# VectorE makes the low weight halves at both ends of a layer, GpSimd scales every second mixer tile, and each product sum takes its high weights first

## What is computed

```python
for l in range(2):
    proj = rmsnorm(x, norm1_g[l]) @ w_in[l]                 # 1024 -> q, k, v, hyena inputs, gates
    a_out = neighbourhood_attention(q, k, v, na_rpb[l])     # 8 heads of 64, with softmax
    u = short_conv(hy_in, ...)                              # width 3, per channel
    b_out = hyena_mixer(u, h_fwd, h_bwd, hy_bias[l])        # long convolutions by spectra
    merged = g0 * (a_out @ w_up_na[l]) + g1 * (b_out @ w_up_hy[l])
    x = x + merged @ w_out[l]
    h = rmsnorm(x, norm2_g[l])
    q = h @ peer_wq[l]; s = q . subkeys                     # scores, top 16 of 128, twice, top 16 of all
    a = gelu(h @ peer_u[l].T)                               # all 16384 experts are computed here
    x = x + (routing weights * a) @ peer_v[l]
```

## Time and profile before

| | us |
|---|---|
| median of 3 runs | 1931.53 |
| lowest and highest | 1929.2 and 1931.96 |
| profiled execution, its own time | 1929.89 |
| its span, first to last instruction | 1927.8 |
| PE busy | 1873.0 (97%) |
| ACT busy | 1355.3 (70%) |
| DVE busy | 1218.7 (63%) |
| POOL busy | 1035.3 (54%) |

### The profile page before, as it was taken

How to read it: one execution, slowest core, us unless ns; L and a number is a source line. 1 busy time by engine, 2 the same in 40 slices (tenths; PEclk the granted TensorE clock), 3 DMA queues, 4 the chain that set the end, 5 groups by cost and what they waited for, 6 DMA issues and landing times.

```text
span 1927.8 us, 42946 instructions
## 1 busy us (share of the span) xinstructions
PE 1873.0 (97%) x14238; PEld 1353.3 (70%) x14238; DVE 1218.7 (63%) x2530; ACT 1355.3 (70%) x1929; POOL 1035.3 (54%) x664
## 2 busy tenths in 40 slices
PE   7989999999999999999989899999999989999999
PEld 5777898899998344444457778988999974444444
DVE  5897569777775344444458974796777744444444
ACT  8787988887777455555588879888877765555554
POOL 4655868876667322222256558687776672222221
PEclk8999999999999999999999999999999999999999
DMA  8544656655555566666565446556555555656654
GB/s 265 164 143 142 214 168 201 202 188 173 174 174 167 173 205 203 200 206 200 192 213 167 143 135 227 173 197 201 192 171 167 173 175 175 206 201 202 206 198 140
DMA packets 100324, 357.38 MB, mean 185 GB/s; under 512 B 11744, under 2 KB 13730, under 8 KB 99492
## 3 DMA queue, kind: packets, MB, share of 16 engines
q1 hardware_dynamic: 99828, 354.36, 55.9%
q10 hardware_dynamic: 432, 2.18, 0.3%
HBM read 355.45 MB, written 1.05 MB: 185 GB/s over the span
## 4 chain that ended last, share of the span: by engine, by line
PE 87%; DVE 6%; ACT 5%; issue 2%; DMA 0%; SPq 0%; POOL 0%; DVEq 0%; ACTq 0%; POOLq 0%
PE bank L1992 35%; PE bank L1536 14%; PE bank L1538 14%; PE bank L1540 14%; PE bank L1931 3%; ACT w_hi L504 2%; ACT ring L510 2%; PE bank L1860 1%; DVE arena L1150 1%; DVE arena L1167 1%; PE bank L1911 1%; PE bank L1865 1%; DVE arena L1146 1%; DVE arena L1148 1%; PE bank L1699 0%
## 5 line engine op out<-in xcount | busy, mean ns | idle before, releaser
L462 POOL TENSOR_TENSOR w_lo<-ring,w_hi 128x1024 f16<-128x1024 f32 x404 | 863.9, 2140 | 396.5 <-ACT ring L510 395.9
L504 ACT ACTIVATE w_hi<-ring 128x1024 f16<-128x1024 f32 x654 | 685.0, 1047 | 38.2 <-PE bank L1540 25.2
L1536 PE MATMUL bank<-act_parts,w_hi 128*128 128x256 f16 x2560 | 698.0, 273 | 0.5 <-DVE act_parts L1268 0.5
L1540 PE MATMUL bank<-act_parts,w_lo 128*128 128x256 f16 x2560 | 697.8, 273 | 0.0
L1538 PE MATMUL bank<-act_parts,w_hi 128*128 128x256 f16 x2560 | 697.7, 273 | 0.0
L897 DVE SCALAR_TENSOR_TENSOR w_lo<-ring,w_hi 128x1024 f16<-128x1024 f32 x250 | 306.3, 1225 | 351.7 <-ACT w_hi L504 351.7
L476 POOL TENSOR_TENSOR e_lo<-arena,e_hi 128x256 f16<-128x256 f16 x256 | 171.2, 670 | 480.9 <-ACT e_hi L813 480.9
L510 ACT ACTIVATE ring<-ring 128x1024 f32<-128x1024 f32 x404 | 424.2, 1050 | 0.0
L1992 PE MATMUL bank<-w_hi,e_hi 128*128 128x512 f16 x1024 | 390.3, 381 | 11.3 <-issue 11.3
L1992 PE MATMUL bank<-w_lo,e_hi 128*128 128x512 f16 x1024 | 390.2, 381 | 0.0
L1992 PE MATMUL bank<-w_hi,e_lo 128*128 128x512 f16 x1024 | 389.9, 381 | 0.0
(11 more groups left out here) (258 smaller groups left out, 1862.1 us busy)
## 6 DMA issues: line engine op xcount, KB each, us to landing
ring<-stream SPq DMA_DIRECT2D x654, 512.0 KB, 3.3
arena<-rpb_in SPq DMA_DIRECT2D x8, 512.0 KB, 6.2
arena<-subkeys ACTq DMA_DIRECT2D x2, 1024.0 KB, 5.6
ring<-stream SPq DMA_DIRECT2D x4, 256.0 KB, 4.8
xT<-x_in SPq DMA_DIRECT2D x4, 256.0 KB, 5.2
arena<-w_in SPq DMA_DIRECT2D x2, 512.0 KB
arena<-decay_in SPq DMA_DIRECT2D x2, 512.0 KB
arena<-dft_in SPq DMA_DIRECT2D x2, 512.0 KB, 4.3
```

The lines of the kernel that those rows point to most:

```text
L462: pool.tensor_tensor(w_lo[:, slot, :], ring[:, slot, :], w_hi[:, slot, :], ALU.subtract).then_inc(lo_ready.sem, 1)
L504: nc.scalar.activation(w_hi[:, slot, :], ring[:, slot, :], ACT.Copy, scale=TABLE_SCALE).then_inc(hi_ready.sem, 1)
L1536: T.matmul(out_, weights(w_hi, tile, j), hi[:, k, :], start=start, stop=False, skip_group_check=True)
L1540: return T.matmul(out_, weights(w_lo, tile, j), hi[:, k, :], start=False, stop=stop, skip_group_check=True)
```

## The change

Three things are changed.

1. **DVE makes the low halves at both ends of a layer.** Tiles 2 to 5 of each layer, and tiles 200 to 203, move from POOL to DVE's one-instruction form, and ACT no longer scales them. DVE's `low_part` for tiles 2 and 3 stands in layer 0 behind the second and fourth `add_squares`, in layer 1 behind the second and fourth `raw_low_pair`; for tiles 4 and 5 behind the sum of squares, ahead of `inverse_rms`. For tiles 200 to 203 it stands among the last three `store_late`. DVE's wait for the low half of tile 203 is gone. POOL begins with tile 6 and ends with tile 199.
2. **POOL scales the odd tiles from 7 to 71 itself.** There it waits for `hi_ready`, scales the tile in place with a `tensor_scalar`, waits for itself, and subtracts. ACT scales 33 tiles fewer in each layer this way. The even tiles from 6 to 70, and all of 72 to 199, stay as they were. That makes 404 scalings on ACT before, 322 after, and 66 new ones on POOL.
3. **`contract` takes high weights first.** It waits for the high half, issues the 16 matmuls with `w_hi` (both activation halves, block by block), then waits for the low half and issues the eight with `w_lo`. The number of matmuls is the same. At tile 4 the mean of squares is behind the wait for the high half, and no longer behind that for the low half.

`lo_ready` is split in `low_by_vector` and `low_by_pool`, each counted in its own order; PE and SP wait for the one of the tile's maker. Loops are cut where the maker changes.

```diff
+VECTOR_HEAD = 6
+def made_by_vector(tile):
+    return tile < VECTOR_HEAD or tile >= T_VT
+def scaled_by_pool(tile):
+    return VECTOR_HEAD <= tile < T_U and tile % 2 == 1
...
+        def low_wait(eng, l, i, tile):
+            made = low_by_vector if made_by_vector(tile) else low_by_pool
+            eng.wait_ge(made.sem, made.at(l, i * RING + lows_by_engine(tile)))
...
-            def scaled_low(l, i, tile):
+            def pool_low(l, i, tile):
                 slot = tile % RING
-                pool.wait_ge(ring_scaled.sem, ring_scaled.at(l, i * RING + (tile + 1 - HEAD)))
+                if scaled_by_pool(tile):
+                    pool.wait_ge(hi_ready.sem, hi_ready.at(l, tile + 1))
+                    scaled[0] += 1
+                    pool.tensor_scalar(ring[:, slot, :], ring[:, slot, :], TABLE_SCALE, None, ALU.mult
+                                       ).then_inc(pool_scaled, 1)
+                    pool.wait_ge(pool_scaled, scaled[0])
+                else:
+                    pool.wait_ge(ring_scaled.sem, ring_scaled.at(l, i * RING + scaled_by_scalar(tile)))
                 pool.tensor_tensor(w_lo[:, slot, :], ring[:, slot, :], w_hi[:, slot, :], ALU.subtract
-                                   ).then_inc(lo_ready.sem, 1)
+                                   ).then_inc(low_by_pool.sem, 1)
             def pool_layer(l):
-                pool.wait_ge(lo_ready.sem, lo_ready.at(l, HEAD))
-                for tile in range(HEAD, RING):
-                    scaled_low(l, 0, tile)
-                with pool.Fori(1, POOL_TILES // RING) as i:
+                for tile in range(VECTOR_HEAD, T_U):
+                    pool_low(l, 0, tile)
+                with pool.Fori(0, NK // RING) as i:
                     for s in range(RING):
-                        scaled_low(l, i, s)
+                        pool_low(l, i, T_U + s)
...
             def scale_tile(tile):
+                if not made_by_vector(tile) and not scaled_by_pool(tile):
...
                         raw_low_pair(b)
                         if not l:
                             head_low(b % 2, b // 2)
+                        elif b % 2:
+                            low_part(l, 0, HEAD + b // 2)
                 for b in range(KT // 2):
                     add_squares(b, pair_sum, bank[6 + b % 2][:, :])
+                    if not l and b % 2:
+                        low_part(l, 0, HEAD + b // 2)
...
+                for tile in range(RING, VECTOR_HEAD):
+                    low_part(l, 0, tile)
                 inverse_rms(1)
...
                 burst(TGROUPS // RING - 1, False)
+                low_part(l, 0, T_VT)
                 store_late(0, LATE - 3)
-                dve.wait_ge(lo_ready.sem, lo_ready.at(l, POOL_TILES))
+                low_part(l, 0, T_VT + 1)
                 for n in range(LATE - EDGE, LATE):
                     store_late(0, n, last_fresh)
+                    low_part(l, 0, T_VT + RING + n - LATE)
...
                 def contract(out_, i, tile, wait=None, parts=(act_hi, act_lo)):
-                    parts_ready(i, tile)
+                    hi, lo = parts
+                    high_ready(i, tile)
                     for k in range(KT):
                         if wait is not None:
                             wait(k)
-                        ins = product(out_, tile, k, k, k == 0, k == KT - 1, parts)
+                        for moving in (hi, lo):
+                            T.matmul(out_, weights(w_hi, tile, k), moving[:, k, :], start=(k == 0 and moving is hi),
+                                     stop=False, skip_group_check=True)
+                    parts_ready(i, tile)
+                    for k in range(KT):
+                        ins = T.matmul(out_, weights(w_lo, tile, k), hi[:, k, :], start=False, stop=(k == KT - 1),
+                                       skip_group_check=True)
                     return ins
```

More of the change, by code:

```diff
@@ L89, with lows_by_engine, scaled_by_scalar @@
 PI_BELOW = 3.1415925
+def made_by_vector(tile):
+    return tile < VECTOR_HEAD or tile >= T_VT
+def scaled_by_pool(tile):
+    return VECTOR_HEAD <= tile < T_U and tile % 2 == 1
+def lows_by_engine(tile):
+    return sum(made_by_vector(t) == made_by_vector(tile) for t in range(tile + 1))
+def scaled_by_scalar(tile):
+    return sum(not made_by_vector(t) and not scaled_by_pool(t) for t in range(tile + 1))
 class Signal:
@@ L272, in encoder_kernel @@
         hi_ready = sig("hi_ready", TILES)
-        ring_scaled = sig("ring_scaled", POOL_TILES - HEAD)
-        lo_ready = sig("lo_ready", TILES)
+        ring_scaled = sig("ring_scaled", scaled_by_scalar(TILES - 1))
+        low_by_vector = sig("low_by_vector", lows_by_engine(TILES - 1))
+        low_by_pool = sig("low_by_pool", lows_by_engine(T_VT - 1))
+        pool_scaled = sem("pool_scaled")
         tile_done = sig("tile_done", TILES)
@@ L365, in load, with refill @@
                              ).then_inc(ring_full[slot].sem, 16)
-            def refill(turn, slot):
-                sp.wait_ge(lo_ready.sem, turn * RING + (slot + 1 - RING))
-                load(turn * RING + slot, slot)
+            def refill(l, i, group, slot):
+                tile = (group - 1) * RING + slot
+                if group:
+                    low_wait(sp, l, i, tile)
+                else:
+                    low_wait(sp, l - 1, i, TILES + tile)
+                load(i * RING + (l * TILES + group * RING + slot), slot)
             def layer_loads(l):
@@ L410, in layer_loads @@
                     for slot in (2 * (r % 2), 2 * (r % 2) + 1):
-                        refill(l * GROUPS + 3 + r // 2, slot)
+                        refill(l, 0, 3 + r // 2, slot)
                         if slot % 2 == 0:
                             offsets(r)
-                with sp.Fori(l * GROUPS + 5, (l + 1) * GROUPS) as turn:
+                with sp.Fori(0, T_VT // RING + 1 - 5) as i:
                     for slot in range(RING):
-                        refill(turn, slot)
+                        refill(l, i, 5, slot)
+                with sp.Fori(0, GROUPS - 1 - T_VT // RING) as i:
+                    for slot in range(RING):
+                        refill(l, i, T_VT // RING + 1, slot)
             def load_x(b):
@@ L509, in scale_tile @@
                 slot = tile % RING
-                nc.scalar.activation(ring[:, slot, :], ring[:, slot, :], ACT.Copy, scale=TABLE_SCALE
-                                     ).then_inc(ring_scaled.sem, 1)
+                if not made_by_vector(tile) and not scaled_by_pool(tile):
+                    nc.scalar.activation(ring[:, slot, :], ring[:, slot, :], ACT.Copy, scale=TABLE_SCALE
+                                         ).then_inc(ring_scaled.sem, 1)
             def head_high(tile, half):
@@ L786, in act_layer @@
                     norm_high(2, (s,))
-                with act.Fori(2, (T_U - T_WQ) // RING) as w:
-                    for s in range(RING):
-                        high_part(l, w, T_WQ + s + RING)
-                        scale_tile(T_WQ + s + RING)
+                for tile in range(T_WQ + 3 * RING, T_U + RING):
+                    high_part(l, 0, tile)
+                    scale_tile(tile)
                 for n in range(8):
@@ L836, in act_layer @@
                     late_gelu(0, n)
-                with act.Fori(0, TGROUPS // RING) as i:
+                with act.Fori(0, TGROUPS // RING - 1) as i:
                     for s in range(RING):
                         late_gelu(i, EDGE + s)
+                for n in range(LATE - EDGE - RING, LATE - EDGE):
+                    late_gelu(0, n)
                 for n in range(LATE - EDGE, LATE):
@@ L908, in head_low @@
                                        w_hi[:, tile, columns], ALU.mult, ALU.subtract
-                                       ).then_inc(lo_ready.sem if half else head_lo[tile], 1)
+                                       ).then_inc(low_by_vector.sem if half else head_lo[tile], 1)
             def dve_layer(l):
@@ L1525, in parts_ready @@
                 def parts_ready(i, tile):
-                    pe.wait_ge(lo_ready.sem, lo_ready.at(l, i * RING + (tile + 1)))
+                    low_wait(pe, l, i, tile)
                 def weights(part_, tile, k):
```

21 lines of the change are left out of this document (9 added, 12 removed).

## The result

The changed kernel takes 1964.22 us, median of 4 runs (1962.53 to 1965.61), against 1931.35 us (1929.2 to 1931.96, 4 runs) of the kernel before: a ratio of 1.0172, 95% interval 1.0154 to 1.0189. I had said 1909, range 1897 to 1926. The profiled execution's span is 1960.6 us, 32.8 more than before.

The account below looks back on a forecast made before the run. PE bounds the dense stages; elsewhere its waits for DVE, ACT or POOL set the end. Gains 16 + 6.6 + 4.8 + 3.8 less 9.6 in attention make 21.6 off 1929.9; forecast 1909 us, range 1897 to 1926.

Parts of the forecast that it names:

- What POOL's scaling costs: One POOL scaling of 128x1024 was taken at 1.16 us, between bounds 1.05 and 2.14; paid in attention and dense stretch.
- the change of sign: Price of one POOL scaling, 1.85 us, above which the whole change was forecast to make the kernel slower.
- the dense formula: Loss in tiles 48 to 71, both layers, at price p per POOL scaling: 24(p - 0.88) - 10; nothing at 1.16.
- the early one: Formula from v tiles to convolution, both layers: attention's loss less 3.8 for other scalings; +5.8 us at 1.16.
- The rival at 2.14: POOL's scaling costs as much as its subtraction, 2.14 us: kernel slower, 1941 us; chance 0.09.
- The dense stretch: Tiles 48 to 71: POOL falls 0.28 us behind PE a pair, 3.4 over 12 pairs, within 5 reserve; cost nothing.
- Attention: DVE's gap-free queue there is slowed by POOL's scaling, 6 odd tiles x 0.8 us; 9.6 us given back in both layers.
- 12(p - 0.36) less 3.8: Attention's loss in both layers at price p per POOL scaling, less the 3.8 us gained by other scalings.
- Between the expert tables: PE's wait before the second table (11.3 us) and half clock after it (5.1) go, but for 0.5: 16 us gained.
- Both starts: Start of each layer up to the v tiles comes earlier: 6.6 us gained in layer 0, 4.8 in layer 1.
- Other scalings on the chain: Behind the v tiles, two odd-tile ACT scalings a layer leave the chain, 4 x 0.95: 3.8 us gained.
- The order of products costs nothing: High weights first in contract costs nothing in the dense stages: the same 24 matmuls, a weight load each.

Follow-up runs that it names:

- the experiment on those tiles alone: Changed kernel with GpSimd scaling only odd tiles 49 to 71 by the one-operation instruction, ScalarE the others: 1945.69 us, 1.0079 to before.
- Every fourth and every eighth tile: Changed kernel with GpSimd scaling, from tile 48 to 71, only every fourth tile (1914.33 us) or every eighth (1908.0 us); ScalarE scales the rest.
- with two operations: Changed kernel whole, GpSimd's scaling made a multiplication and an addition of zero in one instruction: 1920.22 us, 0.9951 to before.
- GpSimd's filler: Kernel without GpSimd scaling plus unused GpSimd work ahead of layer 0's tile 20: subtraction 1914.65, two two-operation instructions 1913.98, one multiplication 1911.26 us.

## Why the prediction was wrong, point by point

- **What POOL's scaling costs** is the step that failed, in its value of 1.16 and in its upper bound. "[T]he upper 2.14, as if one input cost what two do" took an instruction with other work to do for a ceiling. The measured price is 2.80, past the 1.85 at which I had put the change of sign; at 2.80 the forecast's own formulas give 1966 us, against 1964.22 measured. That this is so close is in part luck: the dense formula is 3.8 us short, and the early one is 5.2 us over and has the wrong mechanism, as said below. The rival at 2.14 had the right sign and the right account of the dense tiles, and ended 23 us too low. The Trainium skill (GPSIMD Engine Reference, Engine selection) says one-input work is at roughly line rate. The rows agree for a copy, 1.04, and for two operations, 1.05 (my estimate from the page was 1.03), and disagree for one operation, 2.77: it depends on the form, which that section does not say.
- **The dense stretch** was right as a mechanism: a queue with a reserve. Its formula gives 36 us at 2.80; 39.9 were measured (37.3 in the experiment on those tiles alone), and at 1.08 about 1. Every fourth and every eighth tile came out by the same account.
- **Attention** was mis-formed. 12(p - 0.36) less 3.8 gives 25.5 at 2.80, near the 20.3 measured, which looks like a success; at 1.08 it gives 4.8, and 18.3 were measured. The loss hardly depends on p. By its own account attention should have given back 12 x 2.44 = 29.3 us at 2.80, and it gave back 9.4. Two terms were put at nothing. One is the low halves of the filters, ahead of attention: 3.1 and 3.2 us a layer in the changed kernel, 6.4 and 5.9 with two operations. The other is the clock, which falls after the longer waits: from the v tiles to the convolution TensorE's granted clock was 0.98 and 1.00 before (layer 0, layer 1), 0.95 and 0.94 in the changed kernel, 0.92 and 0.96 with two operations. Over the two stretches that makes the changed kernel lose some 12 us of full clock more than before, an estimate, beside 9 us more in which TensorE stands idle; not all of the former lengthens the kernel. GpSimd is busy for 93% of this stretch in the changed kernel, 71% with two operations and 59% without scaling, so with two operations gaps were left and the loss was still there. That it depends on which instructions of the two engines meet is shown at the filters and only argued for attention. What is lost in attention itself shows in VectorE's scaling of the probabilities, here all sixteen of layer 1, in the changed kernel and then in the one without GpSimd scaling:

```profile
L1213 DVE TENSOR_SCALAR arena<-arena,soft 128x256 f32<-128x256 f32 x16 | 16.6, 1038 | 0.6
```

```profile
L1213 DVE TENSOR_SCALAR arena<-arena,soft 128x256 f32<-128x256 f32 x16 | 10.6, 664 | 0.6
```

  With two operations the assumed 1.16 was nearly met (1.08), and the time was 1920.22, not 1909: with the right price this step alone would have left the forecast 11 us too low, within its range. The Trainium skill (SBUF — State Buffer, Who interferes with whom) says that a VectorE instruction with two SBUF inputs contends with a GpSimd instruction that reads SBUF, and that one with at most one does not, outside VectorE's 2-port performance modes. The low halves of the filters (both inputs in SBUF: 2.62 beside a subtraction) and the product with PSUM (0.68 beside a subtraction) agree. The scaling of the probabilities reads one SBUF tensor and a column, and its mean still went from 664 to 1038 ns; whether it ran in such a mode no run here shows.
- **Between the expert tables**: right, 16.8 measured for 16, the wait 11.7 and the half clock 5.1.
- **Both starts**: right, 5.8 for 6.6 and 4.8 for 4.8. Without GpSimd's scaling layer 1 keeps only 2.9 of its 4.8, so those tiles are where it pays; the version that scales 7, 9 and 11 alone has all 4.8.
- **Other scalings on the chain**, 3.8: not seen by themselves; they are buried in the stretch that lost 20.3.
- **The order of products costs nothing**: right; it gives about 3 us, if anything.

**Still open.** The two changed kernels with two operations in all early odd tiles had times between 1916.4 and 1926.3, wider than any other here, and the time goes with the mean granted clock, 0.995 at the lower end and 0.988 at the upper. Their two traces differ most in layer 1 from the v tiles to the convolution: 137.8 us at a clock of 0.96 in one, 141.5 at 0.93 in the other, with about the same idle time of TensorE (13.9 and 13.2 us). What makes the clock fall in one execution and stay up in the next is open. Why the form with one operation is slow was not looked into either.

## What to carry to other kernels

An unseen price needs an upper bound that is a measurement of that very form: here a second operation that does nothing made the instruction 2.6 times as fast. When work is moved to an engine with spare time, ask who used its idle time; here four short VectorE instructions ran at full speed in a gap of GpSimd. A wait of TensorE can cost more than its length: here 5.3 us of added wait were followed by 2.7 more at a lower clock. In a stretch where a queue feeds the bound engine, compare the two rates over a group of tiles, not the cost of one.

## What the runs showed of the hardware that I had not expected

- On GpSimd a `tensor_scalar` of 128x1024 takes 2.77 us with one operation, whatever the type and buffer, idle chip or busy, and 1.05 with two (f32 alone was measured); a copy takes 1.04, a product of two f32 operands 2.34, a subtraction to 16 bit 2.12.
- A VectorE subtraction of 128x512 with both inputs in SBUF goes from 0.68 to 2.62 us beside a GpSimd subtraction, and to 1.52 beside the form with two operations. Beside the slow multiplication, which moves the same bytes in 2.6 times the time, one takes 1.52 and two keep 0.68. GpSimd's filler stretched as well: 2.12 to 2.58, 2 x 1.05 to 1.48 and 1.36, 2.77 to 3.21.
